# A streaming encoder layer on one core: the mixer step reordered, its decay exponents moved from TensorE to GpSimd

## The reference, cut to what matters

```python
def hgrn2_chunk(S, q, k, v, logf):
    L = q.shape[1]
    b = jnp.cumsum(logf, axis=1)
    inter = jnp.einsum('blhk,bhkv->blhv', q * jnp.exp(b), S)
    causal = jnp.tril(jnp.ones((L, L), dtype=bool))
    diff = b[:, :, None] - b[:, None, :]
    dec = jnp.exp(jnp.where(causal[None, :, :, None, None], diff, -jnp.inf))
    A = jnp.einsum('blhk,bmhk,blmhk->bhlm', q, k, dec)
    intra = jnp.einsum('bhlm,bmhv->blhv', A, v)
    bl = b[:, -1]
    k_dec = k * jnp.exp(bl[:, None] - b)
    S_new = jnp.exp(bl)[..., None] * S + jnp.einsum('blhk,blhv->bhkv', k_dec, v)
    return S_new, intra + inter
```

## Time and profile before

| | |
|---|---|
| median of 3 runs | 1231.38 us (1230.04 to 1234.77) |
| the profiled execution | 1232.34 us, of which 1230.6 us is the span from its first to its last instruction |
| PE busy | 1095.6 us, 89% of the span |
| DVE, ACT, POOL busy | 708.4, 602.1 and 107.1 us |
| mean granted clock of TensorE | 0.947 of full speed |

### The profile page before, as it was taken

How to read it: one execution, slowest core, us unless ns; L and a number is a source line. 1 busy time by engine, 2 the same in 40 slices (tenths; PEclk the granted TensorE clock), 3 DMA queues, 4 the chain that set the end, 5 groups by cost and what they waited for, 6 DMA issues and landing times. The chain is left out here.

```text
span 1230.6 us, 26353 instructions
## 1 busy us (share of the span) xinstructions
PE 1095.6 (89%) x8820; PEld 898.8 (73%) x8821; DVE 708.4 (58%) x1321; ACT 602.1 (49%) x1226; POOL 107.1 (9%) x237
## 2 busy tenths in 40 slices
PE   4789999999999999999949999549999998999936
PEld 3688788977898778977837878337877776777722
DVE  3623555245632565326645665777886674767538
ACT  5634445334553444534453212156876664767433
POOL 0000000000000000000000011120011001100150
PEclk9799999999999999999969999659999999999978
DMA  8632222141222321223226341369999996999565
GB/s 308 226 92 74 80 83 60 36 141 53 67 70 58 95 79 35 65 74 118 83 69 212 103 155 60 127 207 338 394 388 351 319 332 229 365 311 350 188 246 205
DMA packets 202399, 210.53 MB, mean 171 GB/s; under 512 B 15612, under 2 KB 169076, under 8 KB 202036
## 3 DMA queue, kind: packets, MB, share of 16 engines
q1 hardware_dynamic: 183120, 177.25, 43.4%
q0 software_dynamic: 5712, 18.23, 4.1%
q10 hardware_dynamic: 13492, 13.96, 3.2%
HBM read 185.32 MB, written 24.08 MB: 170 GB/s over the span
## 5 line engine op out<-in xcount | busy, mean ns | idle before, releaser
L2019 DVE TENSOR_TENSOR experts_w_lo<-all_raw_more,experts_w_hi 128x2048 fp32r<-128x2048 f32 x48 | 108.4, 2287 | 7.2 <-ACT experts_w_hi L1900 7.2
L2019 DVE TENSOR_TENSOR experts_w_lo<-all_raw,experts_w_hi 128x2048 fp32r<-128x2048 f32 x48 | 109.6, 2284 | 4.9 <-ACT experts_w_hi L1900 4.9
L923 PE MATMUL early_ps_proj<-early_w_hi,early_h_hi 128*128 128x512 f32 x256 | 106.4, 416 | 2.6 <-ACT mixers_decay L756 2.6
L2187 PE MATMUL experts_ps_g<-experts_w_hi,experts_x_hi 128*128 128x512 f32 x256 | 104.5, 408 | 2.2 <-DVE experts_x_lo L2025 2.2
L925 PE MATMUL early_ps_proj<-early_w_hi,early_h_lo 128*128 128x512 f32 x256 | 101.2, 395 | 0.0
L2189 PE MATMUL experts_ps_g<-experts_w_hi,experts_x_lo 128*128 128x512 f32 x256 | 100.9, 394 | 0.0
L924 PE MATMUL early_ps_proj<-early_w_lo,early_h_hi 128*128 128x512 f32 x256 | 100.6, 393 | 0.0
L2188 PE MATMUL experts_ps_g<-experts_w_lo,experts_x_hi 128*128 128x512 f32 x256 | 100.5, 393 | 0.0
L1196 DVE TENSOR_TENSOR mixers_qd_t<-mixers_turned,early_tables 128x128 f32<-128x128 f32 (+1 forms) x36 | 10.1, 281 | 152.7 <-ACT mixers_turned L804 135.4
L1900 ACT ACTIVATE experts_w_hi<-all_raw 128x2048 fp32r<-128x2048 f32 x48 | 91.5, 1911 | 5.2 <-DMA all_raw<-in_W_up_e_dram 4.7
L1900 ACT ACTIVATE experts_w_hi<-all_raw_more 128x2048 fp32r<-128x2048 f32 x48 | 91.6, 1913 | 2.0 <-DMA all_raw_more<-in_W_up_e_dram 1.4
(11 more groups left out here) (358 smaller groups left out, 2687.9 us busy)
## 6 DMA issues: line engine op xcount, KB each, us to landing
all_raw_more<-in_W_down_e_dram SPq DMA_DIRECT2D x128, 256.0 KB, 5.4
all_raw<-in_W_gate_e_dram SPq DMA_DIRECT2D x96, 256.0 KB, 5.4
all_raw<-in_W_up_e_dram SPq DMA_DIRECT2D x96, 256.0 KB, 6.5
all_raw<-in_W_in_dram SPq DMA_DIRECT2D x32, 512.0 KB, 4.9
all_raw<-in_W_ada_dram SPq DMA_DIRECT2D x32, 512.0 KB, 4.7
condition_w_ada_in<-in_W_ada_dram SPq DMA_DIRECT2D x4, 2048.0 KB, 12.7
all_raw_more<-in_W_gate_e_dram SPq DMA_DIRECT2D x32, 256.0 KB, 7.2
all_raw_more<-in_W_up_e_dram SPq DMA_DIRECT2D x32, 256.0 KB, 7.3
```

The source lines that it names most:

```text
L923: pe.matmul(out, xhi, whi, start=(k == 0), stop=False)
L2019: dve.tensor_tensor(w_lo[:, 2 * p:2 * p + 2], raw_pair[p], f32(w_hi[:, 2 * p:2 * p + 2]), ALU.subtract).then_inc(lo_done, 1)
L2187: pe.matmul(out, x_hi[:, k, :], w_hi[:, c, at], start=(k == 0), stop=False)
```

## The change

**Exponents.** The tables, the transposes, the rounding and PE's products with `steps` go away. DVE makes b in place by a running sum along each tile (`run`), nine of them per round, all ahead of the tiles. POOL makes the eight differences of each tile by 15 subtractions (`spans`, 11 for the sample tile), those of tile i + 1 in step i, into one buffer `span` in SBUF. ACT's exponential of index 8 reads b, the other eight are one instruction of 1024 columns on `span`. `span` is single: `spans(i + 1)` waits until `decays(i)` has read it.

**Order.** PE's `turn_out(i - 2)` moves behind the second half of the projection, `condition` behind the scores; the wait quoted above falls away. In ACT's list `decayed_keys` moves to the next step, ahead of `decays`; `copies` moves ahead of `normalise`; the store of an output tile comes a step later. In DVE's list `gated` comes a step later and ahead of `scored`. The sample states are stored by SP instead of ACT.

```diff
-LATE = dict(steps=(len(LEVELS) + 2) * P)
...
+        span = sb("span", [P, 8, P])
...
+            def sample_states(g):
...
+                for c, name in enumerate(("ret", "hgrn")):
+                    sp.dma_start(s.outs[f"state_{name}_sample"][0, 0, bass.ds(head, 1)].rearrange("h k v -> k h v"),
+                                 s_sa[:, c:c + 1, :]).then_inc(ss_stored, 16)
...
+                def spans(i):
+
+                    w = frames(i)
+                    pool.wait_ge(sum_done, n[9] + (i + 1))
+                    pool.wait_ge(exp_done, n[9] + i)
+                    b = log_f[:, at(i):at(i) + w]
+                    pool.tensor_tensor(span[:, 0, 0:w], b[:, w - 1:w].broadcast_to([P, w]), b, ALU.subtract)
+                    for c, h in enumerate(LEVELS, 1):
+                        if 2 * h > w:
+                            continue
+                        pairs = b.rearrange("p (b l) -> p b l", l=2 * h)
+                        out = span[:, c, 0:w].rearrange("p (b l) -> p b l", l=2 * h)
+                        middle = pairs[:, :, h - 1:h].broadcast_to([P, w // (2 * h), h])
+                        pool.tensor_tensor(out[:, :, 0:h], middle, pairs[:, :, 0:h], ALU.subtract)
+                        last = pool.tensor_tensor(out[:, :, h:2 * h], pairs[:, :, h:2 * h], middle, ALU.subtract)
+                    last.then_inc(level_done, 1)
+
+                spans(0)
                 for i in range(NT + 2):
                     if i >= 2:
                         refine(i - 2)
+                    if i + 1 < NT:
+                        spans(i + 1)
...
                 def decays(i):
                     w = frames(i)
-                    act.wait_ge(d_done, n[9] + (i + 1))
+                    act.wait_ge(level_done, n[9] + (i + 1))
                     act.wait_ge(kl_done, n[9] + i)
                     act.wait_ge(ql_done, n[9] + i)
-                    act.activation(decay[:, 8, 0:w], ps_cum[:, 0:w], ACT.Exp)
-                    act.activation(decay[:, 4:8, 0:w], ps_d[:, :, 0:w], ACT.Exp)
...
+                    act.activation(decay[:, 8, 0:w], log_f[:, at(i):at(i) + w], ACT.Exp)
+                    for lo, hi in [(0, 8)] if w == P else [(0, 1), (3, 8)]:
+                        last = act.activation(decay[:, lo:hi, 0:w], span[:, lo:hi, 0:w], ACT.Exp)
                     last.then_inc(exp_done, 1)
...
                     pe.wait_ge(ql_done, n[9] + (i + 1))
-                    pe.wait_ge(exp_done, n[9] + min(i + 2, NT))
                     pe.wait_ge(ah_done, n[9] + i)
...
                     if i == 0:
                         project_sample()
-                    if i == 0 or 1 < i < NT:
-                        exponents(i)
...
-                    if i in (2, 5):
-                        condition(i // 5)
                     if i == NT:
                         next_piece(0, (v_done, n[9] + 9))
                     if 1 <= i <= NT:
                         scores(i - 1)
-                    if i >= NT:
-                        next_piece(i - NT + 1, (exp_done, n[9] + 9))
-                    if i >= 2:
-                        turn_out(i - 2)
+                    if i in (2, 5):
+                        condition(i // 5)
                     if 1 <= i <= NT:
                         retention_scores(i - 1)
                     if 1 <= i < NT:
                         project(i, 1)
+                    if i >= NT:
+                        next_piece(i - NT + 1, (v_done, n[9] + 9))
+                    if i >= 2:
+                        turn_out(i - 2)
                     if 1 <= i <= NT:
                         mix(i - 1)
...
+                def run(i):
+
+                    f = log_f[:, at(i):at(i) + frames(i)]
+                    dve.tensor_tensor_scan(f, s.const("ones", 0, frames(i)), f, 0.0, ALU.mult, ALU.add)\
+                       .then_inc(sum_done, 1)
```

More of the change, by code:

```diff
@@ L73 @@
               k_decay=2 * HEADS, s_decay=2 * HEADS)
-LATE = dict(steps=(len(LEVELS) + 2) * P)
-CONSTS = {**KEPT, **TABLES, **LATE}
+CONSTS = {**KEPT, **TABLES}
 N_KEPT, N_TABLES = sum(KEPT.values()), sum(TABLES.values())
-AT = {name: at for part in (KEPT, TABLES, LATE) for name, at in zip(part, np.cumsum([0, *part.values()]).tolist())}
+AT = {name: at for part in (KEPT, TABLES) for name, at in zip(part, np.cumsum([0, *part.values()]).tolist())}
 def width(i):
@@ L109, in constants @@
     c["own_block"] = m // 32 == l // 32
-    between = lambda ref: ((m > ref) & (m <= l)) | ((m > l) & (m <= ref))
-    c["steps"] = np.stack([m > l, *(between(l // (2 * h) * (2 * h) + h - 1) for h in LEVELS), m <= l], 1)
     c["iota"] = np.broadcast_to(np.arange(NE), (P, NE))
@@ L491, in phase_mixers @@
         gate = sb("gate", [P, 2, NTOK])
-        steps = sb("steps", [P, 9, P], F32R)
-        lf_hi = sb("lf_hi", [P, P], F32R)
-        lf_lo = sb("lf_lo", [P, P], F32R)
+        span = sb("span", [P, 8, P])
         decay = sb("decay", [P, 9, P])
@@ L656, in _ @@
                 with sp.If(g < R - 1):
-                    for u in range(6):
+                    for u in range(4):
+                        load(g + 1, u)
+                    sample_states(g)
+                    for u in range(4, 6):
                         load(g + 1, u)
@@ L837, in decayed_keys, with store @@
                                    scale=kd_col[0:w, 0:1] if w == P else kd_col[0:w, 1:2]).then_inc(kdec_done, 1)
[L839 to L843 removed]
+                def store(i):
+                    w = frames(i)
+                    act.wait_ge(out_done, n[9] + (i + 1))
+                    dst = s.o_scr.rearrange("(c g p) t -> g p c t", c=2, g=HEADS)
+                    act.dma_start(dst[bass.ds(n["round"], 1), :, :, at(i):at(i) + w].rearrange("g p c t -> (g p) c t"),
+                                  o_out[:, i % 2, :, 0:w]).then_inc(o_stored[i % 2], 16)
                 for i in range(NT + 2):
@@ L1150, in _ @@
                     split(u, n[8])
-                log_low(0)
+                dve.wait_ge(logf_done, n[1] + 1)
+                for i in range(NT):
+                    run(i)
                 def state(i):
@@ L1233, in rotary @@
                        .then_inc(rot_done, 1)
-                for i in range(NT + 2):
-                    if i >= 2:
+                for i in range(NT + 3):
+                    if 2 <= i < NT + 2:
                         state(i - 2)
+                    if i >= 3:
+                        gated(i - 3)
                     if 1 <= i <= NT:
                         scored(i - 1)
-                    if i >= 2:
-                        gated(i - 2)
                     if i == 0:
```

103 lines of the change are left out of this document (21 added, 82 removed).

## The result

The changed kernel takes 1186.4 us (median of 4 runs, 1185.12 to 1186.93) against 1230.71 for the kernel before: a ratio of 0.964, with an interval of 0.9605 to 0.9672. The forecast was 1190. The profiled execution took 1186.57 us, 45.8 less than that of before. In PE's timeline the mixers last from the first product behind the wait for `hk` at 69.93 to the output projection's first product at 598.63, so 528.7 us; in the kernel before it is 69.71 to 645.88, 576.2. So 47.5 us come out of the mixers, and the phases behind them lie within 1.5 us of before.

The account below looks back on a forecast made before the run. PE, busy 137.76 of 141.80 us per round, was taken as the bound. Gains 35.3, 2.4, 4.8, 4.9, 1.4, 1.8 less 3.6 and 6.0 gave 41.0: 1232.34 to 1191.3, median 1190; 8-in-10 range 1178 to 1230.

Parts of the forecast that it names:

- likeliest case: POOL's loop of 8.5 us per tile stays hidden behind PE's plain step of 8.62; 1178 to 1198, chance 0.54.
- the sum: Gains and losses on PE over the mixers, adding to 41.0 us, from the profiled 1232.34 to 1191.3.
- The spans: POOL's 15 subtractions per full tile: 15 × 0.195 fixed plus 0.84 for columns, 3.8 us, bounds 2.3 and 5.45.
- estimate of 5.2 us: POOL's subtractions per tile at 2.2 ns per column; no measurable change, 1221 to 1235, chance 0.09.
- The shared port: POOL stands still under DVE operations with two SBUF inputs: 3.3 us per step, bounds 0 and 3.9.
- The margin: In a plain step, POOL's loop of 8.5 us is just hidden behind PE's 8.62, by 0.1 us.
- The sample tile's start: Retention scores 0.9 us later per round, −3.6; clock falls after PE's idle time, 1.5 × 4, −6.0.
- The last round's end: PE's wait of 2.69 us for the norm starts its cause earlier in the new order: gain 1.8 us.
- Step 9: PE's wait of 0.47 us for the masked retention scores is covered by `turn_out`: 3 rounds, gain 1.4 us.
- terms (a) to (c): PE's steps lose the products with `steps`, 35.3 us, the log's transpose, 2.4, and the gap ahead of the exponents, 4.8.
- the change does only half: PE's products leave, but the new order's waits stall 0.3 us 28 times, 8 us: 1198; no chance of its own.

## Why the prediction was right, and where it was not

**The time and the direction** were right: 1190 forecast, 1186.4 measured, inside the likeliest case's own range of 1178 to 1198. Between the two profiled executions the sum has 41.0 us, and 45.8 were measured.

**The spans** came out as the sum had them: fifteen subtractions, 0.36 + 14 × 0.25 = 3.86 us when nothing disturbs them, against 3.8. Its two parts were both off, though. The step from 64 to 128 columns costs 0.11 us, 1.7 ns per column, twice the 0.82 taken from the fills; what is left per operation is 0.14 us, and not 0.195. The two errors cancel, so that the sum came out was luck. The Trainium skill's figure (GPSIMD Engine Reference, 3.1), from which 2.2 ns per column and so the estimate of 5.2 us were worked out, is above the 1.7 ns that this trace shows between 64 and 128 columns; no run here has an operation of 2048 columns.

**The shared port** (term of 3.3 us, bounds 0 and 3.9): in a plain step the spans take from 268.00 to 274.47, 6.47 us, so 2.6 of it, 1.9 by the two long operations and the rest in small delays. The rule of the Trainium skill (SBUF — State Buffer, Who interferes with whom) agrees with this trace: subtractions of 0.29 us last 1.17 and 1.27 under DVE's products of 1.18 and 1.34. The margin was 0.7 us in place of 0.1. The run with longer spans shows that the loop itself was drawn rightly, with its period of 9.95 us and 25.6 us lost.

**The sample tile's start** (−3.6 and −6.0) has the right place, cause and sign. The retention scores stand 9.97 us behind the sample's projection (237.51 to 247.48), before 9.79 (from a projection at 247.88 to 257.67), so 0.2 later and not 0.9. The products behind the wait start at half their rate for 4.0 us (247.72 to 251.71), and not for 2.4 to 3.5, so the fallen clock took 2.0 us per round, and not 1.5.

**The last round's end** (1.8): the wait for the norm fell from 2.69 to 0.91, 1.78.

```profile
583.54 0.41 PE L1026 MATMUL mixers_ps_ot<-all_consts_sb,mixers_normed 128*128 128x128 f32 x2 [0.91 <-ACT mixers_normed L813]
```

The sum left out what came with it: in the kernel before the granted clock behind that wait was 0.50 (windows view, 627 to 633) and the pairs of products of `mix` started 0.43 us apart, in the changed kernel it stayed at 1.00 (581 to 587) and they start 0.22 apart.

**Step 9** (1.4): its wait of 0.47 went, but a wait of 0.65 for ACT's reading of the turned pieces came up behind the next transposes, in three rounds too, so all of it was given back.

**What failed is the reason.** The step that failed reads: "whatever leaves PE's list here shortens the round, as long as no other engine's chain becomes longer than PE's work". I examined one such chain, POOL's, and not the one that was already there. The loop of ACT and DVE took 10.20 us in the kernel before and 10.44 in the run with the old order, and PE's own step with the exponents 9.84. So of the 1.66 us that a plain step lost, the exponents alone would have given nothing, and what terms (a) to (c) booked in such steps, as work and gaps that leave with them, was to be had only since the order took the other loop off PE's path at the same time. The rows had the sign of it: a wait of 0.22 us at the head of the step, 24 times, for DVE's `lf_lo`. I took that for a small cost, worth 4.8 us in all; it was the second loop, arriving at PE last in step after step. The rival "the change does only half" looked at waits that the new order might bring and priced them at 8 us; that the order might be the half which decides was in no rival. The forecast of the time came out because the changed kernel's plain step is PE's own work, as the sum had it (8.55 us against 8.62). That the second loop was out of the way there was luck: the new order did it, and the prediction had not checked it.

## What to carry to other kernels

An engine that is busy for 97% of a stage need not be its only bound: a short wait that comes back in every step, however small, can mean that another loop has the same period, and then work taken off the engine buys nothing until that loop is shortened too. So follow each engine's list around once, from an instruction through those queued behind it to the same instruction of the next tile, and add up the loop before pricing a removal. And where a kernel's experiment changes values, read the stage and not the total.

## What was not expected of the hardware

Where nothing disturbs them, POOL's subtractions of 64 columns start 0.25 us apart whether they lie in one block or in 64 blocks of one column (the first pair above starts at 268.36 and 268.61, and the last pair of tile 1, undisturbed ahead of the sample tile's end, at 245.20 and 245.45), so the shape of the blocks costs nothing that these rows show. The delay goes in both directions: DVE's products with two SBUF inputs took 0.10 and 0.12 us longer (1.18 and 1.34 against 1.08 and 1.22) while POOL was subtracting, about a third of one POOL operation each, and POOL's waiting operation lasted about as long as the DVE product over it (1.17 and 1.27).
